# Hybrid layer and two-layer second block: rank-16 product moved into the gates product, rounded step widths, another order in dilated attention, a third expert slot

## The reference

```python
def gla_mixer(q, k, v, og, lr, wa2, ba, norm_g):          # hybrid layer
    log_alpha = jax.nn.log_sigmoid((lr @ wa2 + ba)) / 16  # lr = 16 columns of h @ w_in, wa2 is 16 x 512
    ...                                                   # chunked linear attention
def nsa_mixer(q, kv, gate, ...):                          # gate = 48 other columns of h @ w_in
    g = jax.nn.sigmoid(gate) ...
def _ssd_mixer(x, ...):                                   # second block, layer 0
    dt = jax.nn.softplus(dt_raw + dt_bias)                # dt_raw = 32 columns of x @ w_in
    ...
def _dilated_attention_mixer(x, ...):                     # second block, layer 1
    # three patterns of windowed attention over 8 heads, merged by their softmax weights, @ w_o
def _hierarchical_moe(x, w_rg, b_rg, w_re, b_re, w_gate, w_up, w_down):   # in both layers
    # 32 experts of hidden width 512, two for each token:
    #   h = silu(xb @ w_gate[e]) * (xb @ w_up[e]);  y = h @ w_down[e]
    # each layer reads all experts' weights: 32 x 3 x 2 MB
```

## Time and profile before

| what | us |
| --- | --- |
| median of 3 runs | 3776.06 (3771.88 to 3785.85) |
| the profiled execution | 3775.06 |
| its span, first to last instruction | 3773.2 |
| TensorE busy | 3136.7 (83%) |
| VectorE, ScalarE, GpSimd busy | 1246.4, 847.7, 443.7 |
| mean granted TensorE clock | 0.883 of full |
| gates stage of the hybrid layer | about 326 to 344 |
| rank-16 stage of the linear attention | about 561 to 614 |
| step widths | about 1813 to 1848 |
| routing and experts of layer 0 | about 2165 to 2741 |
| combine of layer 0; its projection's first instruction follows at 2782 | about 2741 to 2782 |
| dilated attention | about 3011 to 3116 |
| routing and experts of layer 1 | about 3155 to 3730 |

### The profile page before, as it was taken

One profiled execution on the slowest core, in us unless ns is written; L12 is line 12 of the kernel. 1 busy time (PEld: TensorE's weight loads), 2 busy tenths in 40 slices (PEclk: granted clock), 3 DMA queues, 4 the chain that ended last, 5 costly groups with the idle time before them and its releaser, 6 DMA issues. The chain is left out here.

```text
span 3773.2 us, 41467 instructions
## 1 busy us (share of the span) xinstructions
PE 3136.7 (83%) x15811; PEld 2185.5 (58%) x15811; DVE 1246.4 (33%) x1989; ACT 847.7 (22%) x1608; POOL 443.7 (12%) x659
## 2 busy tenths in 40 slices
PE   5978986979998999898697868788759975888884
PEld 4766764857776887788575733333348764333331
DVE  2442733243335333426277420000063354000002
ACT  2423722132213320113412011111121141111111
POOL 0031510000000000000031011111103231111110
PEclk9988997989998999999756978899879996898787
DMA  3232021113322322222001279999832104999995
GB/s 103 89 74 87 2 69 45 46 34 89 89 89 78 100 83 95 85 88 68 2 1 39 92 313 403 396 402 404 322 117 90 62 1 178 361 404 391 389 394 227
DMA packets 249760, 603.59 MB, mean 160 GB/s; under 512 B 39238, under 2 KB 203588, under 8 KB 224941
## 3 DMA queue, kind: packets, MB, share of 16 engines
q1 hardware_dynamic: 238764, 585.22, 42.6%
q0 software_dynamic: 10880, 16.83, 1.3%
HBM read 596.68 MB, written 24.16 MB: 165 GB/s over the span
## 5 line engine op out<-in xcount | busy, mean ns | idle before, releaser
L2367 PE MATMUL bank<-moe_raw,ex_xT 128*64 128x512 f32 x2048 | 556.5, 705 | 158.7 <-DMA moe_raw<-in_moe_w_up 156.5
L276 PE MATMUL bank<-hT_hi,cut_hi 128*128 128x512 f32 x1248 | 502.8, 403 | 65.2 <-DVE cut_lo L296 39.9
L276 PE MATMUL bank<-hT_lo,cut_hi 128*128 128x512 f32 x1248 | 497.0, 398 | 0.0
L276 PE MATMUL bank<-hT_hi,cut_lo 128*128 128x512 f32 x1248 | 496.3, 398 | 0.0
L2367 PEld LDWEIGHTS bank<-moe_raw,ex_xT 128*64 128x64 f32 x2048 | 187.2, 162 | 480.4 <-issue 473.8
L2454 DVE TENSOR_TENSOR ex_h<-ex_gate,bank 64x512 f32<-64x512 f32 x64 | 44.1, 690 | 995.8 <-ACT ex_gate L2417 995.8
L276 PEld LDWEIGHTS bank<-hT_hi,cut_hi 128*128 128x128 f32 x1248 | 239.9, 192 | 123.9 <-DVE cut_lo L1641 26.7
L294 DVE CAST cut_hi<-raw 128x2048 fp32r<-128x2048 f32 (+1 forms) x118 | 119.0, 1009 | 546.2 <-PE bank L276 453.7
L276 PEld LDWEIGHTS bank<-hT_lo,cut_hi 128*128 128x128 f32 x1248 | 240.0, 192 | 54.8 <-issue 1.9
L276 PEld LDWEIGHTS bank<-hT_hi,cut_lo 128*128 128x128 f32 x1248 | 239.3, 192 | 54.1
L276 PE MATMUL bank<-cut_hi,hT_hi 128*128 128x256 f32 x768 | 224.0, 292 | 54.0 <-DVE cut_lo L296 54.0
(11 more groups left out here) (487 smaller groups left out, 4637.5 us busy)
## 6 DMA issues: line engine op xcount, KB each, us to landing
moe_raw<-in_moe_w_gate SPq DMA_DIRECT2D x64, 2048.0 KB, 14.0
moe_raw<-in_moe_w_up SPq DMA_DIRECT2D x64, 2048.0 KB, 18.4
moe_raw<-in_moe_w_down SPq DMA_DIRECT2D x64, 2048.0 KB, 9.5
raw<-in_w_in SPq DMA_DIRECT2D x26, 1024.0 KB, 5.4
raw<-in_w_ffn_in SPq DMA_DIRECT2D x44, 512.0 KB, 5.0
raw<-in_ssd_w_in SPq DMA_DIRECT2D x20, 1024.0 KB, 5.3
raw<-in_attn_w_qkv SPq DMA_DIRECT2D x18, 1024.0 KB, 5.0
raw<-in_w_in SPq DMA_DIRECT2D x24, 512.0 KB, 4.4
```

The source lines that it names most:

```text
L276: last = nc.tensor.matmul(out, a(pa, k), b(pb, k), start=(k == 0 and n == 0), stop=(k == total - 1 and n == len(TERMS) - 1))
L2367: last = nc.tensor.matmul(GU[s][rows, :], xT[:, s, k * ER:(k + 1) * ER], raw[:, s, which, k * HID:(k + 1) * HID], start=(k == 0), stop=(k ...
```

## The change

Four edits. The 16 columns of the linear attention are loaded beside the 48 gate columns and multiplied in the same product (rows 64 to 79 of its result), and the result is kept in `K.lr` until `gla_keys` uses it. The step widths' 32 columns are split and multiplied as rounded products. In dilated attention the turns come three steps after the scores, the ring of probabilities has 8 places, ScalarE copies before both exponentials, and VectorE adds both masks before the reciprocal. The experts get a third slot for expert 2, made of the space of `K.hT` (`K.third`, 32 KB) and of `K.raw`, loaded during routing and used once; experts 3, 4, 5 and so on alternate between the two older slots. Since `K.raw` is in use then, the opening load of the attention's projection moves from the end of the SSD output projection to `moe_combine` of layer 0.

```diff
 def nsa_gates(nc, K, w, gate, bias):
-                sp.dma_start(raw[:, :, :], w[:, :, C_GATE:C_GATE + 48]).then_inc(loaded, 16)
+                sp.dma_start(raw[:, :, 0:48], w[:, :, C_GATE:C_GATE + 48]).then_inc(loaded, 16)
+                sp.dma_start(raw[:, :, LR], w[:, :, C_GLA_LR:C_GLA_LR + 16]).then_inc(loaded, 16)
                 for gp in range(2):
...
+                nc.gpsimd.memset(raw[:, :, 48:LR.start], 0.0).then_inc(gap_set, 1)
...
-                product(nc, K.bank[0][0:48, :], lambda part, k: part_of(cut, part)[:, k, :], lambda part, k: part_of(K.hT, part)[:, k, :],
+                product(nc, K.bank[0][0:LR.stop, :], lambda part, k: part_of(cut, part)[:, k, :], lambda part, k: part_of(K.hT, part)[:, k, :],
...
+                nc.scalar.activation(K.lr[LR, :], K.bank[0][LR, :], ACT.Copy).then_inc(kept, 1)
 def gla_keys(nc, K, A, w, qt, kt, ke, decay):
-                sp.dma_start(wlr[:, :, :], w[:, :, C_GLA_LR:C_GLA_LR + 16]).then_inc(loaded, 16)
-                sp.dma_start(wa2[:, :], A.gla_wa2[0]).then_inc(loaded, 16)
+                sp.dma_start(wa2[LR, :], A.gla_wa2[0]).then_inc(loaded, 16)
...
-                pe.wait_ge(loaded, 32)
-                narrow_product(nc, K.bank[4][0:16, :], wlr, K.hT).then_inc(lr_ready, 1)
-                pe.wait_ge(lr_kept, 1)
+                pe.wait_ge(loaded, 16)
...
-                nc.scalar.activation(lr[:, :], K.bank[4][0:16, :], ACT.Copy).then_inc(lr_kept, 1)
 def ssd_steps(nc, K, A, w, rows):
-                pe.wait_ge(loaded, 48)
-                narrow_product(nc, K.bank[0][0:SH, :], wdt, K.hT).then_inc(made, 1)
+                pe.wait_ge(is_split, 1)
+                product(nc, K.bank[0][0:SH, :], lambda part, k: part_of(cut, part)[:, k, :], lambda part, k: part_of(K.hT, part)[:, k, :], KD).then_inc(made, 1)
...
+                dve.wait_ge(loaded, 48)
+                split_weights(nc, dve, wdt[:, :, :], cut.hi[:, :, :], cut.lo[:, :, :], rounded, 1).then_inc(is_split, 1)
 def ssd(nc, K, A, tail):
-            project_model(nc, K, A.ssd_w_out_2[0], SI // P, yT, tail(late))
+            project_model(nc, K, A.ssd_w_out_2[0], SI // P, yT, tail(late), begin=False)
 def moe_route(...):
+                sp.wait_ge(product_ready, 1)
+                for which in range(3):
+                    sp.dma_start(raw[2][which], weights_d[which][2]).then_inc(K.w_loaded[2][which], 16)
                 sp.wait_ge(x_stored, 16)
 def moe_experts(...):
-                with sp.Fori(1, pairs_used(sp)) as i:
+                def load(b, e, slot, users):
+                    for which, used in ((GATE, gate_up_ready), (UP, gate_up_ready), (DOWN, down_ready)):
+                        sp.wait_ge(used, users)
+                        sp.dma_start(raw[slot][which], weights_d[which][ds(e, 1)].rearrange("e p f -> p (e f)")).then_inc(w_loaded[slot][which], 16)
+
+                load(3, 3, 0, 1)
+                load(4, 4, 1, 2)
+                load(5, 5, 0, 4)
+                with sp.Fori(3, pairs_used(sp)) as i:
                     for s in range(2):
                         b = i * 2 + s
...
+                        load(b, sp.value_load(expert[0:1, ds(b, 1)], min_val=0, max_val=NE - 1), 1 - s, b - 1)
 def moe_combine(nc, K, A, layer, weight, tail):
                 tail.loads(sp)
+                if K.opening:
+                    K.opening.begin(sp)
 def attend_residues(nc, K, masks, qk, v, oT):
-    RING, TURNS = 6, 4
+    RING, TURNS, DELAY = 8, 4, 3
...
-                for step in range(N + 2):
+                for step in range(N + DELAY):
                     if step < N:
                         add_mask(step, 0)
+                        add_mask(step, 1)
                     if 1 <= step < N + 1:
...
-                    if step < N:
-                        add_mask(step, 1)
-                    if step >= 2:
-                        copy_odd(step - 2)
+                    if step >= DELAY:
+                        copy_odd(step - DELAY)
...
-                for step in range(N + 2):
+                for step in range(N + DELAY):
+                    if step >= DELAY:
+                        copy_even(step - DELAY)
                     if step < N:
                         exponentials(step, 0)
-                    if step >= 2:
-                        copy_even(step - 2)
-                    if step < N:
                         exponentials(step, 1)
```

More of the change, by code:

```diff
@@ L277, in product @@
     return last
[L280 to L285, removed]
 def part_of(pair, part):
@@ L498, in _ @@
                 tail.loads(sp)
-                if then:
+                if then and begin:
                     sp.wait_ge(w_split, kt)
@@ L1111, in nsa_gates @@
         sb = lambda n, s: mem.enter_context(nc.sbuf_tensor(f"gates_{n}", s, F32))
[L1112 to L1115, removed]
+        raw, squashed_T, far = sb("raw", [P, KD, LR.stop]), sb("squashed", [48, S]), sb("far", [P, P])
+        cut = Pair(mem, nc, "gates_cut", [P, KD, LR.stop])
+        with stage(nc, "loaded", "gap_set", "rounded", "is_split", "far_set", "product", "squashed", "turned", "kept", "walled") as (
+                block, (loaded, gap_set, rounded, is_split, far_set, product_ready, squashed, turned, kept, walled)):
             @block.sync
             def _(sp):
[L1118 removed]
+                sp.dma_start(raw[:, :, 0:48], w[:, :, C_GATE:C_GATE + 48]).then_inc(loaded, 16)
+                sp.dma_start(raw[:, :, LR], w[:, :, C_GLA_LR:C_GLA_LR + 16]).then_inc(loaded, 16)
                 for gp in range(2):
@@ L2069, in moe @@
         idx, place = sb("idx", [ER, NB + 2], U32), sb("place", [P, NB], U32)
-        K.w_loaded = [[nc.alloc_semaphore(f"w_loaded{layer}_{s}_{which}") for which in range(3)] for s in range(2)]
+        K.w_loaded = [[nc.alloc_semaphore(f"w_loaded{layer}_{s}_{which}") for which in range(3)] for s in range(3)]
         x, y, to = sb("x", [ER, 2, D]), sb("y", [P, 2, HID]), sb("to", [P, 2], U32)
@@ L2076, in moe @@
         with nc.sbuf_tensor(f"moe{layer}_raw", [P, 2, 3, WN], F32) as raw:
+            raw = [[raw[:, s, which, :] for which in range(3)] for s in range(2)] + [[K.third[:, :WN], K.third[:, WN:], K.raw[:, :]]]
             moe_route(nc, K, A, layer, weight, expert, pairs, idx, place, raw, x, y, to)
@@ L2376, in turn_h, with down @@
                     last.then_inc(h_turned, 1)
-                def down(s, i, b):
+                def down(s, b, slot, loaded):
                     pe.wait_ge(h_kept, b + 1)
-                    pe.wait_ge(w_loaded[s][DOWN], i * 16 + 16)
+                    pe.wait_ge(w_loaded[slot][DOWN], loaded)
                     pe.wait_ge(y_kept, b + 1)
@@ L2717, in value @@
                     last.then_inc(valued, 1)
-                for step in range(N + 3):
+                for step in range(N + DELAY + 1):
                     if step < N:
                         score(step)
-                    if 2 <= step < N + 2:
-                        turn(step - 2, 0)
-                    if step >= 3:
-                        value(step - 3)
-                    if 2 <= step < N + 2:
-                        turn(step - 2, 1)
+                    if DELAY <= step < N + DELAY:
+                        turn(step - DELAY, 0)
+                    if step > DELAY:
+                        value(step - DELAY - 1)
+                    if DELAY <= step < N + DELAY:
+                        turn(step - DELAY, 1)
             @block.gpsimd
```

64 lines of the change are left out of this document (36 added, 28 removed).

## The result

The changed kernel takes 3732.34 us, the median of 4 runs (3728.31 to 3743.96), beside 3776.40 for the kernel before on the same chip (4 runs, 3771.88 to 3785.85). The ratio is 0.9887, with a 95% interval of 0.9867 to 0.9908: 44 us less, between 35 and 50, where 39 were forecast.

A forecast was written before the change was run, and what follows sets the result against it. No one bound: transfers pace the expert loop, serial chains the rank-16 stage and step widths, a ring of waits attention. 15 + 8 + 9 + 8 - 1 = 39 us less than 3775.06, so 3737 us by the runs' median, range 3728 to 3745.

The forecast's parts named there:

- gates stage: Gates product with 16 more columns: a loss of 1 us, bounds -2 and -0.5, as the bias lands later.
- rank-16 stage: Linear attention's rank-16 product: a gain of 15 us from removing 32 passes, a copy and two hand-overs.
- dilated attention: Attention steps become bound by TensorE, 4.6 us against 5.52: a gain of 9 us, bounds 3 and 12.
- third slot, both layers: Expert 2's weights loaded during routing: a gain of 4 us in each layer, 8 in all, ends -1 and 26.
- the short runs' share of 0.9 us: Gates stage: the 16-column load in runs of 64 B takes 0.9 us of all DMA engines, delaying the bias that much.
- rival (c): Attention's step is bound by VectorE's masks and copy, stays at 5.3 us or more, gain 0: 3746 us; chance 0.10.
- the growth of the drain: End of dilated attention: a round more, two turns, a `value` and a wait for VectorE's copy, 4.3 us more.
- The late first gather: Before the experts: the first gather meets expert 2's transfer, so the first gate/up starts 6.5 us later, bounds 0 and 7.4.
- The lead: Expert loop: of the 16.3 us of transfers moved into routing, 10.4 remain as gain per layer, bounds 7 and 13.
- Rival (b): Experts: the third slot brings nothing, through late later gathers or longer DMA idle time: 3745 to 3751 us; chance 0.16.
- (a): Experts: the first gather isn't held up, the third slot brings 10.4 us a layer: 3724 us; chance 0.18.
- (d): Expert loop: TensorE stays at the slow clock, each block costs up to 3 us more, slower than before; chance 0.04.

The follow-up runs named there:

- after_gfirst: The changed kernel with one edit: GpSimd gathers block b+3's rows before it scatters block b's results; 3719.89 us in one execution.
- late_third: The changed kernel with the third slot's loads issued only when the first two gathers of rows have landed; 3722.49 us in one execution.
- before_again: The kernel before, unchanged, traced once more to see how far its stages differ between executions; 3781.69 us.

## Why the prediction was right, and where not

The forecast of 39 us was met with 44 (35 to 50 by the interval), but its terms were not all right. A minus is a loss:

| term | forecast | measured (means of the table) |
| --- | --- | --- |
| gates stage | -1 | -0.2, from two samples of before that are 1.0 apart |
| the stages behind it, up to the rank-16 stage, same code | none | -2.2 (217.5 and 218.8 us before, 219.0 to 221.0 after) |
| rank-16 stage | 15 | 15.1 in the profiled pair, 16.3 in the means |
| step widths | 8 | 7.6 |
| SSD scan behind them | none | 2.5 to 6.6, mean 5.2 |
| dilated attention | 9 | 9.7 |
| third slot, both layers | 8 | 2.3 at the end of the experts |
| opening load | 0 | 0: from the combine's first load to the projection's first product 44.2 before, 44.4 after |

With 16.3 for the rank-16 stage these make 38.7. The stretch from the rank-16 stage's end to the step widths adds 3.0 by its means, but both kernels have it short and long (1194.5 and 1203.2 us before, 1193.5 to 1203.3 after), so this is chance as far as is known. The rest up to 44 is within what executions differ by: the terms account for a gain near the forecast, not for each us of the medians.

**Rank-16 and step widths** went as worked out: the last absolute value 9.05 us after the issue (some 9 forecast), ScalarE released after 11.81 (11.5 forecast). The eight `wa2` passes ran at the half clock as assumed, 7.19 us.

**Gates stage.** The step that was priced too high is the short runs' share of 0.9 us, which was to be added to the bias loads. The Trainium skill (DMA: Bandwidth & Descriptors, Specifications), which puts line rate at runs of 512 B and more, was weighed there: the row agreed with it on the load's own duration, but no trace shows that duration added to the transfers behind it. The addition starts at 15.17 us in the mean with the load and at 15.48 and 14.44 without it, and one load for two makes 0.45 to 0.6; so the loss is some tenths of a us, and what it consists of stays open. ScalarE ends at 15.14 us, near the 14.9 of the prediction, and 2.2 us before the addition ends: its extra work is covered. The stage ends at 347.46, past the 346 that was named as a sign against this, but only because it started 4.0 us later in this execution.

**Attention.** The step is bound by TensorE at 4.57 us, as forecast, so rival (c) is out. Steps and fill are right; the growth of the drain was priced at 4.3 us. The added round does take 4.25, but the wait of 0.91 us for ScalarE's copy, which the old drain still had, is gone from it: against the two other traces with the old attention the drain grew by 3.3. In the pair it grew from 22.9 to 24.6, by 1.7, because the profiled drain of before also ran part of its passes at the half clock (a `value` of 2.75 us for 1.53, at a granted clock of 0.66 from 3101 to 3106), which the one of after didn't. The clock of fill and drain differs between executions, which makes the pair's 11.9 a lucky one. What the prediction didn't ask is whether the lag is needed at all.

**Third slot: mis-sized.** The late first gather was priced at 6.5 us (its rows give 9.7 - 3.0 = 6.7) and cost 54.87 - 49.15 = 5.7 in the means of the table. The lead was priced at 10.4 and is 7.0 (from the first gate/up to block 6: 89.4 without, 82.4 with). The step that failed is the sequence by which expert 5's down load goes out at 60.5 and expert 6's weights are there at 79. The turn of block 3 waits about 2 us for gathered rows, and in five of the six traced layers gate/up 3 then takes 1.7 us longer (8.8 for 7.1), at a lower clock: the down load leaves at 61.1 to 63.5, 62.8 in the mean. From there to gate/up 6 it is 19.4 to 19.7 us, where the prediction had 18.5; SP needs 2.2 us from that issue to the next (2265.91 to 2268.08), and its loop with register loads begins there, but no run shows how much of the 1.1 us this makes. 2.3 + 1.1 = 3.4 = 10.4 - 7.0; `after_gfirst`, without the wait for rows, gives 2.8 of it back. Rival (b), that the gathers behind the first are late as well, is thus nearly what happened: 1.1 us a layer remain. The sum came out right because the scan, which the sum doesn't have, gave what the slot withheld.

**Rivals (a) and (d).** The first gather was held up in every traced layer, by 5.7 us in the mean, so (a) is out. The row that spoke for (a), the least gather time of 3.0 us, is that of a gather on an idle machine: in `late_third` the shortest is 2.9 again. What is true of (a) is that the gather didn't wait for the whole load: it landed 4.0 us before expert 2's down part. A block of the loop takes (2695.60 - 2285.36) / 25 = 16.4 us as before (16.3), so (d) is out.

Still open is what makes the scan's clock differ: the two traces with the old stage before it have 0.59, the twelve with the new one more. They go together, but the cause isn't shown: nothing was run that changes the scan's start alone, and with the same stage before it the scan took 164.3 us in some kernels and 168 in others. Nor is it settled why `after_gfirst` ends its experts 7 us earlier than its lead explains.

## What to carry over

A load brought forward into an idle stretch of the DMA engines should be measured against the small transfer that the critical path issues in the same stretch: here 6 MB moved early cost 5.7 us at a gather of some rows, and a wait on that gather gave them back. A buffer that is used once is worth only what the next late resource leaves, so follow the whole chain (rows, scatter order, queue) past the first wait that disappears. Where two edits come together, as lag and order did in attention, try each alone: ScalarE's order brought the gain, the longer lag a loss of 3.6 us. And where a stage of unchanged code differs by up to 10 us between executions, one trace of each kernel can't be compared stage by stage: take several.

## What the runs showed of the hardware

An indirect gather of up to 64 rows lands 2.7 to 3.8 us after its issue on empty DMA engines. From 2140 to 2330, where weights stream most of the time, it is 9.5 to 10.2 us in the median and 11.5 at most (the tile of gathered rows in eight kernels). Here are the changed kernel and `late_third` up to the end of their first gathers' stretch (2140 to 2204, 2140 to 2200):

```profile
DMA to landing us min/median/max: 8.5/9.4/10.3
```

```profile
DMA to landing us min/median/max: 2.9/3.6/9.4
```

TensorE's granted clock in a stage of unchanged code differs between kernels and between executions: the scan with its 600 matmuls took 164.3 us at 0.65, 168.3 at 0.62 and 171.0 at 0.59. In the same way the linear attention after 703.57 ran its first 30 us at a mean clock of 0.58 in the profiled changed kernel, and at 0.89 in the profiled one before:

```profile
703.57:733.57 30.00, 25.91 (x67) 15.78 (x68) 6.57 (x14) 5.38 (x3) 0.00 (x0) 0.58 0.01 3
```

```profile
714.15:744.15 30.00, 25.64 (x106) 16.69 (x107) 10.29 (x22) 7.90 (x12) 0.00 (x0) 0.89 0.01 3
```

Both were busy 26 of 30 us, and did 67 and 106 matmuls. The stretch from 609 to 819 in the changed kernel is 10 us longer than the same code before (210.3 and 200.7 us), a quarter of the effect under study. Only other traces show that the change isn't the cause: `before_again` has 210.0, and the other kernels with the new rank-16 stage 200.3 to 210.2.
